# Split f32r products for the experts' down projection in a hybrid decoder block, on one core

## What is computed

```python
hg = xb @ w_gate_up[e] + b_gate_up[e]
gate = jnp.minimum(hg[:, 0::2], SWIGLU_LIMIT)
up = jnp.clip(hg[:, 1::2], -SWIGLU_LIMIT, SWIGLU_LIMIT)
act = (up + 1.0) * (gate * jax.nn.sigmoid(SWIGLU_ALPHA * gate))
return act @ w_down[e] + b_down[e]
```

## Time and profile before

| | us |
|---|---|
| median of 3 runs | 2150.99 |
| lowest, highest | 2149.54, 2151.02 |
| span of the profiled execution, from the first to the last instruction | 2148.6 |
| PE busy in it | 2034.6 (95%) |
| DVE busy | 1177.3 (55%) |
| ACT busy | 893.5 (42%) |
| POOL busy | 385.0 (18%) |

### The profile page before, as it was taken

One profiled execution on the slowest core, in us unless ns is written; L12 is line 12 of the kernel. 1 busy time (PEld: TensorE's weight loads), 2 busy tenths in 40 slices (PEclk: granted clock), 3 DMA queues, 4 the chain that ended last, 5 costly groups with the idle time before them and its releaser, 6 DMA issues.

```text
span 2148.6 us, 24227 instructions
## 1 busy us (share of the span) xinstructions
PE 2034.6 (95%) x8333; PEld 1465.1 (68%) x8333; DVE 1177.3 (55%) x1233; ACT 893.5 (42%) x890; POOL 385.0 (18%) x385
## 2 busy tenths in 40 slices
PE   7799999999999959999999999999999999999991
PEld 5587787888788547667667667667667667667660
DVE  7255556454301247656656656646646646646634
ACT  5343422333422125545445445445445445445421
POOL 4333354333244011010010010010010010010000
PEclk9899999999999968999999999999999999999996
DMA  5122232222432526898889888888899889888845
GB/s 149 49 79 79 69 81 69 70 75 76 134 98 67 228 104 255 317 323 333 323 324 333 326 321 334 325 320 334 323 318 337 323 318 335 324 316 333 324 148 209
DMA packets 189158, 494.33 MB, mean 230 GB/s; under 512 B 16920, under 2 KB 115296, under 8 KB 155744
## 3 DMA queue, kind: packets, MB, share of 16 engines
q1 hardware_dynamic: 179072, 474.89, 62.7%
q0 software_dynamic: 9360, 16.80, 2.1%
q10 hardware_dynamic: 688, 2.13, 0.2%
HBM read 490.10 MB, written 20.97 MB: 238 GB/s over the span
## 4 chain that ended last, share of the span: by engine, by line
PE 89%; DVE 5%; issue 2%; ACT 1%; DMA 1%; POOL 0%; DVEq 0%; POOLq 0%; ACTq 0%; SPq 0%
PE ps L951 20%; PE ps L938 11%; PE ps L935 11%; PE ps L936 11%; PE ps L678 8%; PE ps L680 8%; PE ps L679 8%; PE ps L858 3%; PE ps L929 1%; PE ps L960 1%; DVE gt L1635 1%; PE ps L810 1%; PE ps L922 1%; PE ps L725 1%; PE ps L736 1%
## 5 line engine op out<-in xcount | busy, mean ns | idle before, releaser
L1629 DVE TENSOR_TENSOR gul<-guw,guh 128x2048 fp32r<-128x2048 f32 x256 | 583.4, 2290 | 418.0 <-ACT guh L1209 418.0
L1209 ACT CAST guh<-guw 128x2048 fp32r<-128x2048 f32 x256 | 488.6, 1910 | 243.4 <-PE ps L938 243.4
L951 PE MATMUL ps<-dnw,actT 128*128 128x512 f32 x1024 | 444.7, 592 | 0.0
L935 PE MATMUL ps<-guh,xTh 128*128 128x512 f32 x1024 | 410.3, 401 | 0.0
L936 PE MATMUL ps<-gul,xTh 128*128 128x512 f32 x1024 | 403.4, 394 | 0.0
L951 PEld LDWEIGHTS ps<-dnw,actT 128*128 128x128 f32 x1024 | 194.6, 190 | 234.2 <-issue 229.6
L532 POOL TENSOR_TENSOR split<-wraw,split 128x1024 fp32r<-128x1024 f32 (+1 forms) x100 | 242.0, 2426 | 416.5 <-ACT split L1014 415.9
L938 PE MATMUL ps<-guh,xTl 128*128 128x512 f32 x1024 | 279.2, 394 | 0.0
L678 PE MATMUL ps<-xh,split 128*128 128x512 f32 x672 | 269.6, 401 | 0.6 <-DVE attT L1459 0.6
L680 PE MATMUL ps<-xh,split 128*128 128x512 f32 x672 | 264.9, 394 | 0.0
L679 PE MATMUL ps<-xl,split 128*128 128x512 f32 x672 | 264.8, 394 | 0.0
(11 more groups left out here) (281 smaller groups left out, 1844.3 us busy)
## 6 DMA issues: line engine op xcount, KB each, us to landing
guw<-in_w_gate_up SPq DMA_DIRECT2D x256, 1024.0 KB, 6.7
dnw<-in_w_down SPq DMA_DIRECT2D x128, 1024.0 KB, 4.9
wraw<-in_w_in SPq DMA_DIRECT2D x84, 512.0 KB, 3.8
guw<-y_rows SPq DMA_DIRECT2D x4, 2048.0 KB, 15.7
hres<-in_x SPq DMA_DIRECT2D x8, 512.0 KB, 6.1
wraw<-in_w_mlstm_out SPq DMA_DIRECT2D x8, 512.0 KB, 3.7
wmix<-in_w_mix_out SPq DMA_DIRECT2D x8, 512.0 KB, 6.8
wraw<-in_w_attn_out SPq DMA_DIRECT2D x8, 256.0 KB, 2.8
```

The lines of the kernel that those rows point to most:

```text
L935: mm(ps[:, GUB + n, :], xTh[:, k, :], guh[k % 4][:, cols], start=False, stop=False)
L951: last = mm(ps[:, DNB + n, :], actT[:, k, :], dnw[:, k, n * BANK:(n + 1) * BANK], start=False, stop=(k == KD - 1))
L1209: nc.scalar.copy(guh[k % 4][:], guw[:, k, :]).then_inc(gu_rounded, 1)
L1629: tt(gul[:, k, :], guw[:, k, :], guh[k % 4][:], ALU.subtract).then_inc(gu_split, 1)
```

## The change

- `down` takes three f32r products for each chunk and bank, of `actTh` and `actTl` (rounded part and rest of the activations) and of `dnh` and `dnl` (of the weights). For `dnh` the four buffers `guh` are used again, two chunks of 1024 columns in each; `dnl` is written over `dnw`.
- ACT rounds the down weights (`round_down` and its two forms that first wait for `gu_used`), DVE makes their rest (`down_rest`), after TensorE has used chunks 4 to 7 of gate_up. `round_chunk` for chunks 0 to 3 of the next expert now waits for `dn_used`, pair by pair, and stands after `rows` on ACT, ahead of `weighted`.
- DVE makes the rest of the activations (`act_rest`).
- ACT reads the gates in PSUM: Relu(7 - g) into `gt`, and then the sigmoid of it with scale -1.702 and a bias of 1.702 x 7. DVE's own cut of the gates goes; one instruction cuts and multiplies.
- TensorE's `slots_of(e + 2)` moves to the middle of `gate_up(e)`, behind chunk 3. On DVE `selected(e + 2)` moves between the rests of chunks 5 and 6, and `select` moves from behind chunk 7 to the end of the turn before: `select(e + 3)` behind `act_rest(e)`, ahead of the rests of chunks 2 and 3 of the next expert.

```diff
-            def gate_up(e, xi, gi):
+            def gate_up(e, xi, gi, midway=lambda: None):
...
+                    if k == 3:
+                        midway()
...
                     if k % 2 == 0:
-                        pe.wait_ge(dn_in[k // 2], DMA * (gi + 1))
+                        pe.wait_ge(dn_split, (KD // 2) * gi + k // 2 + 1)
                     for n in range(2):
-                        last = mm(ps[:, DNB + n, :], actT[:, k, :], dnw[:, k, n * BANK:(n + 1) * BANK], start=False, stop=(k == KD - 1))
+                        cols = slice(n * BANK, (n + 1) * BANK)
+                        dnh = guh[k // 2][:, (k % 2) * D + n * BANK:(k % 2) * D + (n + 1) * BANK]
+                        mm(ps[:, DNB + n, :], actTh[:, k, :], dnh, start=False, stop=False)
+                        mm(ps[:, DNB + n, :], actTh[:, k, :], dnl[:, k, cols], start=False, stop=False)
+                        last = mm(ps[:, DNB + n, :], actTl[:, k, :], dnh, start=False, stop=(k == KD - 1))
...
             def expert_turn(e):
-                gate_up(e, e, e)
-                pe.wait_ge(actT_ready, 2 * e)
-                slots_of(e + 2)
+                def next_slots():
+                    pe.wait_ge(actT_ready, 2 * e)
+                    slots_of(e + 2)
+
+                gate_up(e, e, e, next_slots)
                 rows_T(e + 2, e + 1)
                 down(e - 1, e - 1)
                 act_rows_T(e, e + 1)
...
-            def round_chunk(gi, k):
+            def round_chunk(gi, k, before=2):
 
                 sc.wait_ge(gu_in[k], DMA * (gi + 1))
-                if not isinstance(gi, int) or gi or k >= 4:
+                if k >= 4:
                     sc.wait_ge(gu_used, KD * gi + k - 3)
+                elif isinstance(gi, int) and gi == 1:
+                    sc.wait_ge(gu_used, k + 5)
+                elif not isinstance(gi, int) or gi:
+                    sc.wait_ge(dn_used, (KD // 2) * (gi - before) + k + 1)
                 nc.scalar.copy(guh[k % 4][:], guw[:, k, :]).then_inc(gu_rounded, 1)
...
+            def round_down(gi, j):
+
+                sc.wait_ge(dn_in[j], DMA * (gi + 1))
+                nc.scalar.copy(guh[j][:], dnw[:, 2 * j:2 * j + 2, :].rearrange("p k n -> p (k n)")).then_inc(dn_rounded, 1)
+
+            def round_down_behind(gi, j):
+
+                sc.wait_ge(gu_used, KD * (gi + 1) + j + 5)
+                round_down(gi, j)
...
             def sigmoid(gi):
-                sc.wait_ge(gt_ready, gi + 1)
-                a(sg[:], gt[:], ACT.Sigmoid, scale=SWIGLU_ALPHA).then_inc(sg_ready2, 1)
+
+                sc.wait_ge(gu_used, KD * (gi + 1))
+                a(gt[:], ps[:, 0:4, :].rearrange("p b (n c) -> p c (b n)", c=2)[:, 0, :], ACT.Relu,
+                  scale=-1.0, bias=seven[:, 0:1]).then_inc(under_ready, 1)
+                sc.wait_ge(under_ready, gi + 1)
+                a(sg[:], gt[:], ACT.Sigmoid, scale=-SWIGLU_ALPHA, bias=seven[:, 1:2]).then_inc(sg_ready2, 1)
...
                 for k in range(4, KD):
                     round_chunk(e, k)
-                if not last:
-                    for k in range(3):
-                        round_chunk(e + 1, k)
+                if not first:
+                    for j in range(3):
+                        round_down_behind(e - 1, j)
                 sigmoid(e)
+                if not first:
+                    round_down_behind(e - 1, 3)
                 rows(e + 1)
                 if not last:
-                    round_chunk(e + 1, 3)
+                    for k in range(4):
+                        round_chunk(e + 1, k)
                 if not first:
                     weighted(e - 1, e - 1)
                 act_rows(e)
...
+            def down_rest(gi, j):
+
+                dve.wait_ge(dn_rounded, (KD // 2) * gi + j + 1)
+                tt(dnl[:, 2 * j:2 * j + 2, :].rearrange("p k n -> p (k n)"), dnw[:, 2 * j:2 * j + 2, :].rearrange("p k n -> p (k n)"),
+                   guh[j][:], ALU.subtract).then_inc(dn_split, 1)
+
+            def act_rest(gi):
+
+                for b, bank in enumerate((7, 6)):
+                    dve.wait_ge(actTh_ready, 2 * gi + b + 1)
+                    part = (slice(None), slice(4 * b, 4 * b + 4))
+                    tt(actTl[part], ps[:, bank, :].rearrange("p (k c) -> p k c", k=4), actTh[part], ALU.subtract).then_inc(actT_ready, 1)
 
             def swiglu(gi):
                 dve.wait_ge(sg_ready2, gi + 1)
-                own.step(tt(gt[:], gt[:], sg[:], ALU.mult))
+                stt(gt[:], hg[:, 0, :], SWIGLU_LIMIT, sg[:], ALU.min, ALU.mult).then_inc(up_read, 1)
+                dve.wait_ge(up_read, gi + 1)
                 stt(act[:], up[:], 1.0, gt[:], ALU.add, ALU.mult).then_inc(act_ready, 1)
 
-            def expert_turn(e, last=False):
-                for k in range(4, KD):
+            def expert_turn(e, first=False, last=False):
+                for k in range(4, 6):
                     chunk_rest(e, k)
-                select(e + 2, iota_slot)
+                if not first:
+                    selected(e + 2, e + 2)
+                for k in range(6, KD):
+                    chunk_rest(e, k)
+                if first:
+                    select(e + 2, iota_slot)
+                else:
+                    for j in range(3):
+                        down_rest(e - 1, j)
+                ups_in(e)
+                if first:
+                    selected(e + 2, e + 2)
+                swiglu(e)
+                if not first:
+                    down_rest(e - 1, 3)
+                rows(e + 1)
                 if not last:
                     for k in range(2):
                         chunk_rest(e + 1, k)
-                gates_in(e)
-                selected(e + 2, e + 2)
-                ups_in(e)
-                rows(e + 1)
-                swiglu(e)
+                act_rest(e)
                 if not last:
+                    select(e + 3, iota_slot)
                     for k in range(2, 4):
                         chunk_rest(e + 1, k)
```

More of the change, by code:

```diff
@@ L144, in hybrid_block @@
     iota_slot = router.tensor("iota_slot", [P, P])
+    after_gffn = Region(nc, router.at, router.at + D * 4)
     gffn = router.tensor("gffn", [P, D])
@@ L244, in hybrid_block @@
     gul = rests.tensor("gul", [P, KD, F2], F32R)
+    dnl = rests.tensor("dnl", [P, KD, D], F32R)
     dnw = exp_ring.tensor("dnw", [P, KD, D])
@@ L252, in hybrid_block @@
     up = ex.tensor("up", [P, F])
-    actT = ex.tensor("actT", [P, KD, P])
+    actTh = ex.tensor("actTh", [P, KD, P], F32R)
     yw = ex.tensor("yw", [P, D])
@@ L281, in hybrid_block @@
            chunk_b.tensor("guh2", [P, F2], F32R), ex.tensor("guh3", [P, F2], F32R)]
+    actTl = after_gffn.tensor("actTl", [P, KD, P], F32R)
+    seven = ex.tensor("seven", [P, 2])
     ctx = ExitStack()
@@ L328, in hybrid_block @@
         gu_rounded, gu_split, xTh_ready = sem("gu_rounded"), sem("gu_split"), sem("xTh_ready")
+        dn_rounded, dn_split, actTh_ready, seven_ready, under_ready = (
+            sem(n) for n in ("dn_rounded", "dn_split", "actTh_ready", "seven_ready", "under_ready"))
         gu_in = [sem(f"gu_in{s}") for s in range(KD)]
         dn_in = [sem(f"dn_in{s}") for s in range(KD // 2)]
-        gu_used, dn_used, te_ready, sel_ready, meta_mm, meta_ready, gathered, xg_T, xT_ready, up_read, gt_ready, sg_ready2, act_ready, act_T, actT_ready, gcur_ready, y_ready, y_stored = (
+        gu_used, dn_used, te_ready, sel_ready, meta_mm, meta_ready, gathered, xg_T, xT_ready, up_read, sg_ready2, act_ready, act_T, actT_ready, gcur_ready, y_ready, y_stored = (
             sem(n) for n in ("gu_used", "dn_used", "te_ready", "sel_ready", "meta_mm", "meta_ready", "gathered", "xg_T", "xT_ready",
-                             "up_read", "gt_ready", "sg_ready2", "act_ready", "act_T", "actT_ready", "gcur_ready", "y_ready", "y_stored"))
+                             "up_read", "sg_ready2", "act_ready", "act_T", "actT_ready", "gcur_ready", "y_ready", "y_stored"))
         all_stored, gfin_in, f_sum, f_square, f_std, o_ready, o_stored = (
             sem(n) for n in ("all_stored", "gfin_in", "f_sum", "f_square", "f_std", "o_ready", "o_stored"))
-        pool_over, dve_over, act_over = sem("pool_over"), sem("dve_over"), sem("act_over")
+        pool_over, act_over = sem("pool_over"), sem("act_over")
         y_in = [sem(f"y_in{i}") for i in range(NT)]
@@ L586, in _ @@
             own.step(g.memset(tbl[:, E:E + 2, :, 1:4], 0.0))
+            own.step(g.memset(seven[:, 0:1], SWIGLU_LIMIT))
+            g.memset(seven[:, 1:2], SWIGLU_ALPHA * SWIGLU_LIMIT).then_inc(seven_ready, 1)
             g.memset(xg[:], 0.0).then_inc(late_ex, 1)
@@ L1215, in rows, with round_down_behind_own @@
                     nc.scalar.copy(xTh[:, 4 * b:4 * b + 4, :].rearrange("p k c -> p (k c)"), ps[:, bank, :]).then_inc(xTh_ready, 1)
[L1217 to L1219 removed]
+            def round_down(gi, j):
[4 more added lines that the diff above has]
+                round_down(gi, j)
```

(40 more changed lines are left out.)

## The result

| | median, us | ratio to before, 95% interval |
|---|---|---|
| before | 2150.81 | |
| the changed kernel | 2273.79 (2271.47 to 2276.13) | 1.0574 [1.0559, 1.0589] |

The profiled execution of the changed kernel spans 2269.7 us, 121.1 us more than before. The change is slower, as forecast, but by 123 us and not by 79, which lies 6 us above the range.

What follows compares the result with a forecast made beforehand. TensorE's own work was taken to bound the kernel. From 2148.6 us, -81.5 (down), -5.1 (idle), +118.5 (stalls), +0.9 and +0.6 (last, first turn), +46 (clock) gave 2228 us of span; with 2.4 more 2230 us, range 2169 to 2268.

Steps and rivals of the forecast that it cites:

- Direction and mechanism: Slower, chance 0.90: POOL's late table holds `select` on DVE and the rest of chunk 2, so TensorE idles in gate_up.
- The gain of the down product: Three f32r products in place of float32 give 2.63 us in each of 31 down products inside turns: -81.5 us.
- The stall term: TensorE idles 3.95 us ahead of chunk 2 of gate_up, in 30 turns: +118.5 us.
- The turn without a stall: TensorE's own minimum for a turn with all waits covered: 37.4 us.
- the clock term: TensorE's clock falls in the stalls, losing 0 to 1.8 us a turn: 44 us, +46 with the last turn.
- the share: Part of the 54 us clock loss taken, 0.82, by how near 3.95 us idle is to 1.50 and 4.49.
- The rival that the clock stays high: TensorE keeps its clock in most stalls, each being shorter than the one that lost it: 2184 us, chance 0.22.
- POOL held up by DVE: POOL's second operation in the stall's chain is slowed beside `act_rest`, stall 1.2 us longer: 36 us, 2266 us, chance 0.10.
- The faster rival: POOL's table comes before `select` needs it, stall 1.2 us: about 2102 us; chance 0.08, shared with all waits covered, 2064.
- The last turn: The last down product waits for copy, rounding and split of the activations: +0.9 us, and 2 us for the clock.
- The first turn's +0.6: In the first turn Relu precedes a table load and the sigmoid, and the rows' rest follows the activation: +0.6 us.

Runs made afterwards that it cites:

- e2: The changed kernel with POOL's copy of the table of expert e + 3 moved ahead of the scatter: 2104.79 us, 0.979.
- e4: The changed kernel with `select` moved behind the rests of chunks 2 and 3 on DVE: 2087.07 us, 0.9707.
- e3: The changed kernel with `weighted` and the activations' casts moved ahead of the cast of chunk 3 on ACT: 2170.45 us, 1.0095.
- e7: The changed kernel with 8 filling bfloat16 products put into the stall between chunks 1 and 2 of gate_up: 2211.88 us, 1.0292.
- e1: The changed kernel with 16 filling bfloat16 products put into the stall between chunks 1 and 2 of gate_up: 2197.87 us, 1.0223.
- e5: The changed kernel with `select` behind the rests of chunks 2 and 3, and `weighted` and `act_rows` ahead of chunk 3's cast; the best version: 2065.81 us, 0.961.

## Why the prediction missed

- **Direction and mechanism were right.** The chain `yw`, `sidx`, scatter, gather, `te`, `select`, rest of chunk 2 was named with its times, and the stall is 4.0 us against 3.95. Run e2 took the table out of the chain and the long stall went; run e4 took `select` out of TensorE's way and it went too.
- **The gain of the down product was right**: a piece of 12 products takes 2.78 us, and the version without stalls has a span 82.9 us under the kernel before, worked out as 86.6 without the first and last turns.
- **The stall term** was 118.5 us, 3.95 a turn. A turn without clock loss is 41.64 us against the 37.35 of the best version, 30 x 4.29 = 129 us, so the term was 10 us short. Chunk 2 started 0.2 us later than worked out, most of it a longer wait for `gcur`, and the first product behind a stall is followed after 0.34 us and not after 0.23 (run e2, 1312.43 and 1312.77). The turn without a stall was 0.06 us shorter than forecast, which gives 2 us back.
- **The step that failed is the clock term**: "3.95 us at the low level lose ... 1.8 us", "By how near 3.95 is to either row ... I take 44 us". Measured 2.7 us a turn in every turn once the turns are steady, 80 us in all. Both halves were wrong. The price came from the one row with a fall, where the low level lasted 4 us behind the resumption; here it lasts 6 us. Windows (length, PE busy, granted clock, DMA share, GB/s), first at the end of the first turn in the kernel before, where TensorE resumed at 838.55, and then at the stall of the changed kernel, where it resumed at 1418.12, show that the low level itself was as long in both:

```profile
834.00:835.60 1.60, 0.06 (x1) 1.00 1.00 425
835.70:842.40 6.70, 3.85 (x13) 0.50 0.20 62
842.50:845.00 2.50, 2.50 (x12) 1.00 0.00 0
...
1414.10:1417.30 3.20, 0.01 (x1) 1.00 0.92 341
1417.40:1424.10 6.70, 5.98 (x14) 0.50 0.40 165
1424.30:1428.00 3.70, 3.70 (x22) 1.00 0.83 292
```

  What differed is how much of it fell into the idle stretch, where it costs nothing: 2.9 us before and 0.7 us here. Only the part behind the resumption is paid, at the 0.46 us per us that the prediction had: 6.1 x 0.46 = 2.8 us here, and 3.4 x 0.46 = 1.6 us in run e3. And the share came from a line between two idle lengths, 1.50 and 4.49 us, as if length decided; runs e3 and e7 show it doesn't (1.91 us idle lost the clock in 25 of 29 turns, 2.27 us in 10). By span, 42 us were missed: 36 are this, 8 are the longer turn, and 2 went the other way because the profiled run reached the first experts 2 us earlier. The range went wrong at the same place: it took 1.8 us a turn as the upper end of the clock's price, though one row can't be an upper end.
- The Trainium skill (TensorE: Matmul & The Clock Gate, HAM oscillation) tells of a loop that restarts slow in every turn. With 4.0 us stalls the trace agrees, the clock is lost in every turn; with 1.9 and 2.3 us it was lost in some turns only, and with 1.0 us in none. A loss in every turn would have made the sum 54 us for 44, still under the 80 measured, since the price per stall was too low.
- **The rival that the clock stays high** fell in the trace. Run e1, where the clock does stay high, took 2198 us, against the 2184 us that this rival gave.
- **POOL held up by DVE** fell: POOL's second operation ran at 1410.93 beside `actTl` and took its 0.19 us. That is the form with one operand in PSUM, which no row of before showed; the Trainium skill's rule (SBUF — State Buffer, SBUF: two separate sides) agrees. The other side of the rule shows in run e5, where POOL's work falls beside DVE's rests of chunks, which have both operands in SBUF, and takes 1.63 and 2.12 us for 0.19:

```profile
1331.40 4.48 DVE L1679 TENSOR_TENSOR gul<-guw,guh 128x2048 fp32r<-128x2048 f32 x2
...
1332.10 1.63 POOL L610 COPY gidx<-idx_of 128x1 int32 x1
1333.82 2.12 POOL L611 TENSOR_TENSOR pool_tick<-pool_tick 128x1 f32<-128x1 f32 x1
```

- **The faster rival** did not hold for this kernel, because the table was late. Its price was right: 2102 us was given, and run e2, which makes its condition true, took 2105.
- **The last turn**: from the start of the last transposes to the `yw` behind the last down product (2205.34 to 2225.34) it took 20.0 us against 16.96 before, +3.0; forecast were +0.9 and 2 for the clock. The first turn's +0.6 was of the right size: from the first slot products to the first transposes of activations it took 7.64 us (829.82 to 837.46) against 6.76 before, +0.9.

## What to carry to other kernels

When work is moved, follow every wait that moves with it to the queue of the other engine: `select` was cheap where it stood, and four comparisons of 0.2 us cost 4 us a turn because the table they read stands behind a scatter on POOL. Put waits for late results at the end of what the bounding engine wants, and give the bounding engine's feeders their order by due time. And price an idle TensorE twice, once for the stretch and once for the clock behind it: in this kernel 1.0 us was free of the second price, 1.9 us paid 1.5 us in 25 of 29 turns and 2.3 us in 10 of 29, and 4.0 us paid 1.2 to 2.8 us every time.

## What was not expected of the hardware

Two stalls of one length can cost different amounts: at 4.0 us, with turns of 44.0 and 44.7 us alternating, TensorE resumed at the low level in one turn and at the high level, to fall later, in the next. The changed kernel, with equal turns, met its dear case every time; with 26 us of full-rate products added, a cheaper case came every other turn, and the products cost 3 us. And products put in a stall for nothing but the clock's sake made the changed kernel 76 us faster.
